# Softmax sums of an attention phase by one-column matmuls, with two accumulators and joint context units

## The reference, cut to what matters

```python
def block_attention(q, k, v, scale):
    ...
    def one_block(qi):
        s = jnp.einsum('bqhgd,bkhd->bhgqk', qi, k, preferred_element_type=F32) * scale
        p = jax.nn.softmax(s, axis=-1).astype(v.dtype)
        return jnp.einsum('bhgqk,bkhv->bqhgv', p, v)
```

## Time and profile before

| | us |
|---|---|
| runs of the kernel | 4702.43 median of 3 (4701.08 to 4705.49) |
| profiled execution, device time | 4697.07 |
| its span in the profile | 4695.3 |
| TensorE busy | 3868.4 (82% of the span) |
| VectorE busy | 2325.0 (50%) |
| ScalarE busy | 1217.1 (26%) |
| GpSimd busy | 582.4 (12%) |
| mean granted TensorE clock | 0.858 of 2.4 GHz |

### The profile page before, as it was taken

How to read it: one execution, slowest core, us unless ns; L and a number is a source line. 1 busy time by engine, 2 the same in 40 slices (tenths; PEclk the granted TensorE clock), 3 DMA queues, 4 the chain that set the end, 5 groups by cost and what they waited for, 6 DMA issues and landing times. The chain is left out here.

```text
span 4695.3 us, 48023 instructions
## 1 busy us (share of the span) xinstructions
PE 3868.4 (82%) x19902; PEld 2040.8 (43%) x19902; DVE 2325.0 (50%) x3670; ACT 1217.1 (26%) x1598; POOL 582.4 (12%) x340
## 2 busy tenths in 40 slices
PE   7697348788998879999997696359799985999996
PEld 6455235522234545555553454347222332444443
DVE  1782666557662443333334683665567625333334
ACT  1321224323331221111112221232233313221211
POOL 0000321024440000000000000310055400000000
PEclk7898665579998889999998797665699997999998
DMA  4110003110002211111100210022000021111110
GB/s 169 46 40 0 1 1 137 34 26 18 1 1 81 72 54 41 41 41 41 41 32 36 55 40 0 1 83 88 22 14 1 1 72 36 53 52 52 49 48 36
DMA packets 207627, 194.29 MB, mean 41 GB/s; under 512 B 9719, under 2 KB 174386, under 8 KB 206770
## 3 DMA queue, kind: packets, MB, share of 16 engines
q1 hardware_dynamic: 203250, 182.84, 12.5%
q10 hardware_dynamic: 4160, 8.39, 0.5%
HBM read 167.48 MB, written 14.68 MB: 39 GB/s over the span
## 5 line engine op out<-in xcount | busy, mean ns | idle before, releaser
L324 PE MATMUL mlp_acc<-hh,mlp_w 128*128 128x512 f16 (+1 forms) x3840 | 753.7, 359 | 53.4 <-DVE mlp_w L314 53.4
L324 PE MATMUL mlp_acc<-mlp_aa,mlp_w 128*128 128x512 f16 (+1 forms) x3840 | 749.2, 358 | 0.0
L324 PEld LDWEIGHTS mlp_acc<-hh,mlp_w 128*128 128x128 f16 x3840 | 376.8, 98 | 428.3 <-DVE mlp_w L314 54.3
L324 PEld LDWEIGHTS mlp_acc<-mlp_aa,mlp_w 128*128 128x128 f16 x3840 | 375.7, 98 | 371.2
L324 PE MATMUL in_acc<-hh,in_w 128*128 128x512 f16 (+1 forms) x2088 | 401.4, 355 | 70.2 <-DVE in_w L314 57.7
L1423 DVE TENSOR_REDUCE at_mx<-at_small 128x1 f32<-128x512 f32 (+1 forms) x600 | 334.8, 591 | 244.8 <-PE at_small L1480 157.9
L1373 POOL TENSOR_TENSOR at_accp<-at_accp,at_p 128x1024 f32<-128x1024 f32 x144 | 339.1, 2355 | 264.2 <-ACT at_p L1403 259.4
L1403 ACT ACTIVATE at_p<-at_sT 128x1024 f32<-128x1024 f32 (+1 forms) x252 | 252.9, 1004 | 440.5 <-PE at_sT L1508 440.4
L647 DVE SCALAR_TENSOR_TENSOR yf<-mlp_acc,yf 128x1280 f32<-128x1280 f32 (+1 forms) x112 | 152.0, 1357 | 398.6 <-PE mlp_acc L324 398.6
L634 DVE TENSOR_TENSOR mlp_r<-mlp_r 128x1280 f32<-128x1280 f32 (+1 forms) x64 | 86.9, 1358 | 477.0 <-ACT mlp_r L615 477.0
L324 PEld LDWEIGHTS in_acc<-hh,in_w 128*128 128x128 f16 (+1 forms) x2088 | 208.5, 101 | 261.2 <-DVE in_w L314 58.5
(11 more groups left out here) (262 smaller groups left out, 4899.3 us busy)
## 6 DMA issues: line engine op xcount, KB each, us to landing
mlp_stage<-in_w_ff SPq DMA_DIRECT2D x128, 512.0 KB, 4.0
pa_wada<-in_w_ada SPq DMA_DIRECT2D x16, 2048.0 KB, 8.3
in_stage<-in_w_in SPq DMA_DIRECT2D x36, 512.0 KB, 4.2
set_wada<-in_w_ada ACTq DMA_DIRECT2D x4, 2048.0 KB, 19.8
out_stage<-in_w_out SPq DMA_DIRECT2D x16, 512.0 KB, 5.3
nf_wada<-in_w_ada SPq DMA_DIRECT2D x4, 2048.0 KB, 8.0
x<-x_scratch SPq DMA_DIRECT2D x1, 5120.0 KB, 17.4
xin<-in_x SPq DMA_DIRECT2D x8, 512.0 KB, 6.1
```

The costliest lines, as they stand in the source:

```text
L324: last = self.nc.tensor.matmul(acc[0:mw, a:a + c], w[:, wh, k, m0:m0 + mw], src[:, sh, k0 + k, a:a + c], start=(k == 0 and wh == 0 and sh ...
```

## The change

- **Units.** A class `Unit` holds a unit's parts. The context queries of two pairs (four heads) form one unit of 512 columns; layer 0 now has the order long, long, long, long, context: 12 long and 3 context units. The eight maxima of a context unit stand with those of the unit after it.
- **Sums.** VectorE's `accd` is added into `accp` by GpSimd (an eighth addition in a long unit), so one accumulator holds all. A new small task "sum" makes eight matmuls with a 128x128 part of `accp` as the stationary operand and one column of `ones`: they leave the sums of 2 heads x 4 tiles of queries in 8 columns, queries on partitions. VectorE takes the reciprocal of 128x8.
- **Broadcast.** A new small task "bc" makes eight matmuls with one column of the reciprocals, repeated to 64 columns, against the identity, which puts the reciprocals along the queries on all rows of each head. VectorE copies this from PSUM to `o32`, and multiplies by `acc`. Both tasks stand behind the maxima of their step: the sum at step 3 and the broadcast at step 5 of the next unit, or at the first and second step of the long unit behind, where a context unit comes next.
- **Accumulators.** `acc` has two buffers of one bank each; values of a unit wait for the product of the unit before last. ScalarE's copy to `po` is gone.
- **High and low part.** ScalarE casts the high part (at step 7 of the next unit), GpSimd subtracts for the low part (behind its addition of step 8).
- **Queries.** `qq` and `qs` have three buffers for the pairs.

```diff
+QRING = 3
+class Unit:
+    def __init__(self, parts, kts):
+        self.kts, self.parts, at = kts, [], 0
+        for pr, tok, n in parts:
+            self.parts.append((pr, tok, at, n))
+            at += n
+        self.long = len(kts) > 2
+        self.keys = chunks(len(kts) * P)
...
-    for pr in range(6):
-        units += [(pr, 0, 512, list(range(TT))), (pr, 512, 512, list(range(TT)))]
+    for a in range(0, 6, 2):
+        units += [Unit([(pr, q0, 512)], list(range(TT))) for pr in (a, a + 1) for q0 in (0, 512)]
         if full:
-            units.append((pr, LAT, CTX, [TT - 2, TT - 1]))
+            units.append(Unit([(pr, LAT, CTX) for pr in (a, a + 1)], [TT - 2, TT - 1]))
...
-            finish_at[u, 8] = [v for v in range(long[k - 1] if k else 0, u)]
+        for u in range(U):
+            end = base[u + 1] - 1
+            soon = u + 1 < U and not units[u + 1].long
+            want.setdefault(end + (3 if soon else 4), []).append(("sum", u))
+            want.setdefault(end + (4 if soon else 6), []).append(("bc", u))
...
-        qq, qs = sb("qq", [P, 2, 2, TOK], F16), sb("qs", [65, 2, 2, TOK], F16)
+        qq, qs = sb("qq", [P, QRING, 2, TOK], F16), sb("qs", [65, QRING, 2, TOK], F16)
...
-        po, rc, o32 = sb("po", [P, 3, 2, 512]), sb("rc", [P, 512]), sb("o32", [P, 512])
+        rc, o32 = sb("rc", [P, 2, 8]), sb("o32", [P, 2, 512])
-        acc = ps("acc", [P, 2, 512])
+        acc = [ps(f"acc{i}", [P, 512]) for i in range(2)]
...
             @block.gpsimd
+                def low(u):
+                    pool.wait_ge(s_hi, u + 1)
+                    nc.gpsimd.tensor_tensor(result(u, 1), scaled(u), result(u, 0), ALU.subtract).then_inc(s_lo, 1)
...
+                            pool.wait_ge(s_pacc, adds_p[i] - 1)
+                            if longs[i]:
+                                pool.wait_ge(s_dacc, adds_d[i])
+                                other = accd[:, :, :]
+                            else:
+                                pool.wait_ge(s_p, i + 1)
+                                other = p32[:, i % PRING, :, :]
+                            nc.gpsimd.tensor_tensor(to, to, other, ALU.add).then_inc(s_pacc, 1)
+                    while done < U and base[done + 1] + 8 <= i:
+                        low(done)
+                        done += 1
...
             @block.scalar
-                    nc.scalar.activation(po[:, u % 3, :, 0:n], acc[:, :, 0:n], ACT.Copy).then_inc(s_po, 1)
+                def high(u):
+                    act.wait_ge(s_read, u + 1)
+                    nc.scalar.activation(result(u, 0), scaled(u), ACT.Copy).then_inc(s_hi, 1)
...
+                    while done < U and base[done + 1] + 7 <= i:
+                        high(done)
+                        done += 1
...
             @block.vector
-                    ch(nc.vector.reciprocal(rc[:, 0:n], po[:, u % 3, 1, 0:n]))
-                    ch.wait(dve)
-                    nc.vector.tensor_tensor(o32[:, 0:n], po[:, u % 3, 0, 0:n], rc[:, 0:n], ALU.mult).then_inc(s_read, 1)
-                    dve.wait_ge(s_read, u + 1)
-                    ch(nc.vector.tensor_copy(hi, o32[:, 0:n]))
-                    ch.wait(dve)
-                    ch(nc.vector.tensor_tensor(lo, o32[:, 0:n], hi, ALU.subtract))
+                        elif kind == "sum":
+                            dve.wait_ge(s_small, j + 1)
+                            nc.vector.reciprocal(rc[:, u % 2, :], sm[j % 2][:, 0:8]).then_inc(s_rc, 1)
+                        elif kind == "bc":
+                            dve.wait_ge(s_small, j + 1)
+                            if u >= 2:
+                                dve.wait_ge(s_lo, u - 1)
+                            nc.vector.tensor_copy(o32[:, u % 2, :], sm[j % 2][:, :]).then_inc(s_bcast, 1)
+                            dve.wait_ge(s_bcast, u + 1)
+                            dve.wait_ge(s_pv, base[u + 1])
+                            nc.vector.tensor_tensor(o32[:, u % 2, :], o32[:, u % 2, :], acc[u % 2][:, :], ALU.mult)\
+                              .then_inc(s_read, 1)
...
             @block.tensor
+                        elif kind == "sum":
+                            pe.wait_ge(s_pacc, adds_p[base[u + 1] - 1])
+                            for par in range(2):
+                                for q in range(4):
+                                    last = nc.tensor.matmul(out[:, 4 * par + q:4 * par + q + 1],
+                                                            accp[:, u % 2, par, q * P:(q + 1) * P], e.ones[:, 0:1],
+                                                            start=True, stop=True)
+                        else:
+                            pe.wait_ge(s_rc, u + 1)
+                            for q in range(4):
+                                for par in range(2):
+                                    last = nc.tensor.matmul(out[64 * par:64 * par + 64, q * P:(q + 1) * P],
+                                                            rc[:, u % 2, 4 * par + q:4 * par + q + 1].broadcast_to([P, 64]),
+                                                            e.ident[:, :], start=True, stop=True)
...
-                    if s == 0 and u:
-                        pe.wait_ge(s_po, u)
+                    if s == 0 and u >= 2:
+                        pe.wait_ge(s_read, u - 1)
...
-                    if final:
-                        pe.wait_ge(s_pacc, adds_p[i])
-                        both = n == 512
-                        for par in range(2):
-                            last = nc.tensor.matmul(acc[64 * par:64 * par + 64, 1, 0:n], e.ones[:, 0:64],
-                                                    accp[:, u % 2, par, 0:n], start=True, stop=not both)
-                        if both:
-                            pe.wait_ge(s_dacc, adds_d[i])
-                            for par in range(2):
-                                last = nc.tensor.matmul(acc[64 * par:64 * par + 64, 1, 0:n], e.ones[:, 0:64],
-                                                        accd[:, par, 0:n], start=False, stop=True)
-                        last.then_inc(s_sum, 1)
```

More of the change, by code:

```diff
@@ L1248, in maxes @@
     def maxes(u):
-        pr, q0, n, kts = units[u]
-        return [("max", u, par, q, c) for q in range(n // P) for c in range(len(chunks(len(kts) * P))) for par in range(2)]
-    finish_at = {}
+        return [("max", u, par, q, c) for q in range(4) for c in range(len(units[u].keys)) for par in range(2)]
     def plan():
-        for t in maxes(0):
-            put((-1, 0), t)
-        for par in range(2):
-            put((-1, 0), ("row", 0, par))
+        want = {}
+        first = [t for t in maxes(0)] + [("row", 0, par) for par in range(2)]
         for k, u in enumerate(long):
@@ L1376, in _ @@
+                    while done < U and base[done + 1] + 8 <= i:
+                        low(done)
+                        done += 1
+                while done < U:
+                    low(done)
+                    done += 1
             @block.scalar
             def _(act):
[L1378 to L1386 removed]
@@ L1453, in _ @@
                                                 ALU.add).then_inc(s_dacc, 1)
-                    maxima((u, s))
-                    for v in finish_at.get((u, s), []):
-                        finish(v)
-                for v in range(finished, U):
-                    finish(v)
+                    tasks(i)
+                tasks(N)
             @block.tensor
@@ L1488, in tasks @@
                             pe.wait_ge(s_neg, u + 1)
-                            if pr < 4 and (pr, "q") not in loaded:
-                                pe.wait_ge(s_load[pr % 2], per_pair * (pr // 2 + 1))
-                                loaded.add((pr, "q"))
-                            for q in range(n // P):
+                            for q in range(4):
+                                pr, _ = units[u].tile(q)
+                                if pr < 4 and (pr, "q") not in loaded:
+                                    pe.wait_ge(s_load[pr % QRING], per_pair * (pr // QRING + 1))
+                                    loaded.add((pr, "q"))
+                                R = shift_row(pr, par)[1]
@@ L1513, in weighted @@
                     u, s = steps[i]
-                    pr, q0, n, kts = units[u]
-                    final = s == len(kts) - 1
+                    kts = units[u].kts
                     pe.wait_ge(s_p, i + 1)
-                    if s == 0 and u:
-                        pe.wait_ge(s_po, u)
-                    for par in range(2):
-                        last = nc.tensor.matmul(acc[64 * par:64 * par + 64, 0, 0:n], value(pr, par, kts[s]),
-                                                p32[:, i % PRING, par, 0:n], start=(s == 0), stop=final)
@@ new lines, in weighted @@
+                    for pr, tok, c, n in units[u].parts:
+                        for par in range(2):
```

(13 more changed lines are left out.)

236 lines of the change are left out of this document (121 added, 115 removed).

## The result

The changed kernel is slower, by less than half of what was forecast: 4714.2 us median against 4699.4, ratio 1.0038 with the interval 1.0025 to 1.0050. A second set of runs gave 4710.1 against 4699.0, 1.0023 (1.0008 to 1.0039). So the change costs 11 to 15 us where 37.5 was forecast, and both medians lie in the range. The median of all runs of before is 3 us under that of the three runs shown ahead of the prediction.

A forecast was written before the change was run, and what follows sets the result against it. TensorE's own sequence was taken as the limit. Sums and broadcast +101.3, tails +2, removed sums -40.2, removed finish -43.7, context units -7.4 gave +12.0; clock +25.5 made +37.5 us, forecast 4740 us, range 4690 to 4795.

The forecast's parts named there:

- What bounds the kernel: In both attention phases TensorE's own sequence is the limit, busy 391 of 440 and 363 of 399 us.
- Removed sums and finish: Long and context units: dropping the old sums saves 40.2 us, dropping VectorE's finish, where TensorE waited, 43.7 us.
- New sums and new broadcast: Steps 3 and 5 of the next unit: 2.3 and 1.75 us of TensorE, in 25 units +101.3 us.
- Context units: Three joint units cost 17.2 us where six cost 24.5: -7.4 us, with as many maxima as before.
- the 2.6 us booked for the old context units' own sums: Six old context units: removing their sums, a quarter of a long unit's each, saves 2.6 us.
- Tails: Behind each layer's last exponential: about 1 us longer, twice, +2 us.
- The clock: At the sums and the stall ahead of the broadcast: 12 and 10 falls for 7, 1.7 us each, +25.5 us.
- A: Rival, chance 0.18: clock falls stay at 7, as most units run through the present stall at full clock; +12, 4714 us.
- B: Rival, chance 0.12: the clock falls at both sums and broadcast in every unit, 50 falls for 7; 4788 us.
- D: Rival, chance 0.08: VectorE's new product waits for GpSimd, 2.09 us for 0.69, TensorE stands in step 6; 4775 us.
- C: Rival, chance 0.14: faster, sums and broadcast hide in idle time at 2.66 us a unit, falls as before; 4680 us.
- The Trainium skill's formula for loads: Broadcast: 53 ns per 64-column load; if 16 loads hid behind nothing, 0.85 us longer each, total 21 us later.

The follow-up runs named there:

- GpSimd's nine additions: Changed kernel with VectorE's addition of tiles 4 and 5 given to GpSimd: 4671.0 us, 0.9942 of the kernel before.
- the wide sums: Changed kernel with sums by ones as stationary operand, as before, over one accumulator at step 8 of the next unit, no broadcast: 4664.8 us, 0.9930 of before.
- The version with neither: Changed kernel with VectorE's addition given to GpSimd, sums by ones over 512 columns without broadcast, and context maxima spread over four units: 4611.7 us, 0.9808 of before.
- the experiment on the reciprocal: Kernel before with its reciprocal over 8 columns in place of 512: 4665.0 us, 0.9925 of before.

## Why the prediction was right in sign and wrong in size

**What bounds the kernel: right.** TensorE's sequence sets the time in both kernels, and what was given to GpSimd and ScalarE cost nothing in the units.

**Removed sums and finish: right in time, wrong in kind.** In the long units the second step is 2.52 us, the first 2.62, and no first step stands for 8 us on VectorE. But the 13.96 us of the earlier trace rows, which I read as TensorE waiting, are in part the lower clock, and the two steps behind them, which I took to run at it, have a clock of 1.00. The window over the two long steps, in the kernel before:

```profile
1096.90:1110.86 13.96, 9.50 (x33) 2.49 (x31) 9.00 (x17) 3.07 (x3) 2.77 (x2) 0.76 0.00 0
```

A clock of 0.76 over 13.96 us is 6.8 us at 0.50, and the other three such places have 6.8 us each too. So of the 43.7 us not 6.6 are clock, as the prediction has it (3.2 in these places and 3.4 in layer 1), but 4 x 3.4 + 3.4 = 17.0. The forecast then had 12.0 + 17.0 = 29.0 us of work and 25.5 - 17.0 = 8.5 of clock, against 6.9 and 11.7 measured. **The work is what failed, not the clock.**

**New sums and new broadcast: this is the step that failed.** I had 2.3 and 1.75 us, together 4.05; the trace shows 1.79 and 1.15, together 2.94. The loads have the price of the earlier trace rows, and the matmuls of the broadcast run two heads side by side, 1.09 us in all, as taken. What did not come on top is the waiting. In the sums it was to be 0.3 us for a maximum and 0.2 for a start, and is nothing. In the broadcast it was to be 0.45 and 0.2, and is 0.1: the maximum that held its buffer had 256 columns and took VectorE 0.42 us, not 0.69, and TensorE made the third maximum meanwhile. In 25 units that is 28 us too much; and only 24 pairs of these tasks stand in the phases, as the last two units of layer 0 are summed in its tail, so there it is 101.3 for 70.6, 31 us. I gave 3.6 us per unit as the point below which the change is faster; at an unchanged clock it would by this term alone have gained 16 us.

**Context units: a second, smaller one.** "The maxima are as many as before" holds for the sum and not for the place. The unit ahead of a joint context unit has 32 in eight steps, and a step of four waits on VectorE: in the changed kernel's first execution (ScalarE, layer 0)

```profile
1099.50 1.02 ACT L1456 ACTIVATE at_p<-at_sT 128x1024 f32<-128x1024 f32 x1 [1.39 <-PE at_sT L1573]
1103.21 1.02 ACT L1456 ACTIVATE at_p<-at_sT 128x1024 f32<-128x1024 f32 x1 [2.69 <-PE at_sT L1573]
```

3.71 us for a step that elsewhere takes 2.63. Two such units are 35.4 and 35.5 us long at the full clock, 4.4 over the others, of which 1.9 are their added rows: 2 x 2.6 = 5 us. The third joint unit ends its layer; the unit ahead of it prepares no long one and takes 29.5. The unit behind the first context unit is 34.4 us with the sums and broadcast of two units, 0.5 more than their price. The joint unit itself costs what was taken (5.68 + 2.01 + 1.99). And the 2.6 us booked for the old context units' own sums were not there to be gained: behind such a unit the first steps took 2.47 and 2.52 us in the kernel before, no more than the 2.62 and 2.52 without any sums now.

**Tails:** 4.5 us, not 2. With these, the work of the forecast becomes 29.0 - 31 + 5 + 0.5 + 2.6 + 2.5 = +9, against 2.4 + 4.5 = 6.9 measured. The last 2 us stay unexplained; they are less than what the estimate of work and clock leaves open.

**The clock: right in kind, and in size as far as one can tell.** I had 22 falls where the sixth steps have 7, and those at the finish gone; counted in the phases are 24, 18 and 17 falls, some of them longer than 3.4 us, against 13 and 12. As time the clock costs 11.7 us on the mean of the profiles for 8.5, and 21.3 in the first pair. The reason given is shown for both places: the sums start falls by themselves (GpSimd's nine additions, where no wait is left), and so does the wait at the sixth step (the wide sums, where no one-column sums are left). The version with neither has no fall. Wrong was to treat it as one number: the same unit has a fall in one execution and none in the next, with the same instructions. What decides that is not shown.

**The rivals.** The median, 4714, is A's number, but not by A's path: A had +12 of work and no clock. Measured are about 7 of work and 4 to 12 of clock. So its number came out by luck: it has the forecast's work, which is 22 us too much, and leaves the new falls out. B's picture, a fall at both places, holds for six units in a row of the second layer in the first execution, and for three in the second. D fell (no product over 0.69 us). C's size for the work (2.66 a unit) was nearer than the forecast's 4.05, but C counted the falls as unchanged.

The Trainium skill's formula for loads (TensorE: Matmul & The Clock Gate, LDWEIGHTS), which would have made the broadcast 0.85 us dearer if the 16 loads hid behind nothing, did not come into play: the trace has 16 loads and 16 matmuls together in 1.09 us, so the loads ran beside the matmuls.

## What to carry to other kernels

A matmul of one column is not cheap where its stationary operand is loaded for it, and it costs a second time, since it does not hold the clock: 1.57 us of such work a unit were worth 53 us, about a third of it clock. A wait of the engine that bounds the time can have the same double price: it had in the experiment on the reciprocal, and hardly in the one without the sixth step's wait, 38 of whose 41 us are work. So look first for the waits in its timeline: two edits that took waits away, and sums over 512 columns, made the changed kernel 100 us faster. When you read a long step as waiting, look at the granted clock over it too: a part of it may be the clock, and belongs in another term of the sum. And where small tasks of one kind are gathered, their number in the fullest step decides, not their total.

## What was not expected of the hardware

- Two executions of one kernel can differ by 14.7 us in a phase with the same instructions: the second phase took 400.3 and 385.6 us, with 57.9 and 23.9 us at the lower clock, while the first phase took 433.4 both times. The difference begins in the phase's first unit, 34.6 us long in one and 29.4 in the other.
- The clock can fall in one unit after another: five consecutive units of the changed kernel's second layer took 34.2, 34.2, 34.2, 34.1 and 34.1 us in its first execution; in the second, the first three of them took 31.03.
- A reciprocal of 8 columns takes 0.21 us on VectorE, one of 512 takes 3.34; GpSimd's subtraction of 128x512 with an f16 result takes 1.16 us, half of its addition of 128x1024.
